# One small fp32 product of the identity (16 columns) in front of runs of feature-major products

## What is computed

```python
# first block, for each of 2 layers
z = rmsnorm(x, norm1_g[i]) @ w_in[i] + b_in[i]          # mq, mk, mv, mo, ..., rq, rk, rv, rg, gm, gr
merged = sigmoid(gm) * (y_m @ w_bm[i]) + sigmoid(gr) * (y_r @ w_br[i])
x = x + merged @ w_out[i]
h2 = rmsnorm(x, norm2_g[i])
x = x + square(relu(h2 @ w_ff1[i] + b_ff1[i])) @ w_ff2[i] + b_ff2[i]
# second block, expert part, for each of 2 layers; 128 * 128 experts
q = (x @ w_q).reshape(B, T, 8, 2, 64)
s = einsum('bthcd,hcnd->bthcn', q, sub_keys)
top_s, top_i = top_k(s, 16); best_s, pos = top_k(all pairs of sums, 16)
h = gelu(x @ exp_u[idx]); out = (softmax(best_s) * h) @ exp_v[idx]
```

## Time and profile before

| | |
|---|---|
| median of 3 runs | 3293.87 us (3293.05 to 3303.98) |
| span of the profiled execution | 3294.1 us |
| TensorE busy | 3190.2 us, 97% |
| VectorE busy | 2158.7 us, 66% |
| ScalarE busy | 1499.6 us, 46% |
| mean granted clock of TensorE | 0.988 |
| DMA | 565.12 MB, mean 172 GB/s |

### The profile page before, as it was taken

One profiled execution on the slowest core, in us unless ns is written; L12 is line 12 of the kernel. 1 busy time (PEld: TensorE's weight loads), 2 busy tenths in 40 slices (PEclk: granted clock), 3 DMA queues, 4 the chain that ended last, 5 costly groups with the idle time before them and its releaser, 6 DMA issues.

```text
span 3294.1 us, 49471 instructions
## 1 busy us (share of the span) xinstructions
PE 3190.2 (97%) x20642; PEld 2822.8 (86%) x20642; DVE 2158.7 (66%) x3111; ACT 1499.6 (46%) x1717; POOL 504.0 (15%) x278
## 2 busy tenths in 40 slices
PE   8999999999999999989999999999999989999998
PEld 7797889797977897877999989888769989989887
DVE  6775665577766655675987755555687977655555
ACT  6444454463434545613444444444344444444443
POOL 0000000000000000010866600000004856300000
PEclk9999999999999999999999999999999999999999
DMA  5454645444545454303544475555424544565553
GB/s 219 157 190 164 225 170 192 155 157 173 192 166 205 179 191 181 116 28 116 179 164 155 145 257 191 192 193 195 173 90 152 182 141 154 203 219 191 192 192 127
DMA packets 87656, 565.12 MB, mean 172 GB/s; under 512 B 10192, under 2 KB 10208, under 8 KB 23568
## 3 DMA queue, kind: packets, MB, share of 16 engines
q1 hardware_dynamic: 80496, 534.81, 45.4%
q0 software_dynamic: 6944, 27.21, 2.5%
HBM read 552.54 MB, written 9.44 MB: 171 GB/s over the span
## 4 chain that ended last, share of the span: by engine, by line
PE 45%; DVE 13%; ACT 2%; issue 1%; DVEq 0%; ACTq 0%
PE bank L2006 14%; PE bank L2033 7%; PE bank L2034 7%; PE bank L2038 7%; PE bank L1987 3%; DVE hid L2774 1%; DVE hid L2737 1%; PE bank L1730 1%; PE bank L1704 1%; PE bank L1731 1%; PE bank L1710 1%; PE bank L1705 1%; PE bank L1738 1%; DVE topi L2743 1%; DVE topi L2734 1%
## 5 line engine op out<-in xcount | busy, mean ns | idle before, releaser
L2162 ACT ACTIVATE w_hi<-raw 128x2048 fp32r<-128x2048 f32 x291 | 557.7, 1917 | 746.1 <-PE bank L2038 376.6
L2439 DVE TENSOR_TENSOR w_lo<-raw,w_hi 128x2048 fp32r<-128x2048 f32 x222 | 508.7, 2292 | 549.2 <-ACT w_hi L2162 548.4
L987 DVE TENSOR_TENSOR w_lo<-raw,w_hi 128x2048 fp32r<-128x2048 f32 x200 | 458.1, 2292 | 337.3 <-ACT w_hi L748 336.0
L748 ACT ACTIVATE w_hi<-raw 128x2048 fp32r<-128x2048 f32 x201 | 384.8, 1916 | 454.1 <-PE bank L521 316.5
L2006 PE MATMUL bank<-act_hi,w_hi 128*128 128x256 f32 x2048 | 497.8, 284 | 0.0
L2006 PE MATMUL bank<-act_lo,w_hi 128*128 128x256 f32 x2048 | 493.1, 282 | 0.0
L2033 PE MATMUL bank<-w_hi,c_hi 128*128 128x512 f32 x1024 | 398.6, 389 | 0.0
L2034 PE MATMUL bank<-w_hi,c_lo 128*128 128x512 f32 x1024 | 398.6, 389 | 0.0
L2006 PEld LDWEIGHTS bank<-act_lo,w_hi 128*128 128x128 f32 x2048 | 389.4, 190 | 0.1
L2006 PEld LDWEIGHTS bank<-act_hi,w_hi 128*128 128x128 f32 x2048 | 389.3, 190 | 0.1
L1627 POOL TENSOR_TENSOR w_lo<-raw,w_hi 128x2048 fp32r<-128x2048 f32 x70 | 332.5, 4757 | 335.3 <-ACT w_hi L2162 174.0
(11 more groups left out here) (507 smaller groups left out, 5299.5 us busy)
## 6 DMA issues: line engine op xcount, KB each, us to landing
raw<-weights SPq DMA_DIRECT2D x492, 1024.0 KB, 4.8
row<-rows POOLq DMA_DIRECT2D x48, 256.0 KB, 4.2
spill<-staged SPq DMA_DIRECT2D x32, 256.0 KB, 3.0
hid<-spill SPq DMA_DIRECT2D x32, 256.0 KB, 4.9
y<-w_pe POOLq DMA_DIRECT2D x2, 1024.0 KB, 5.1
ln_row_mix<-ln_rows POOLq DMA_DIRECT2D x4, 512.0 KB, 4.9
hid<-keys POOLq DMA_DIRECT2D x2, 1024.0 KB, 6.2
ln_row_ffn<-ln_rows POOLq DMA_DIRECT2D x4, 512.0 KB, 6.7
```

The source lines that it names most:

```text
L748: nc.scalar.activation(w_hi[:, k % SPLIT, :], raw[:, k % RAW, :], ACT.Copy).then_inc(hi_ready, 1)
L987: nc.vector.tensor_tensor(w_lo[:, k % SPLIT, :], raw[:, k % RAW, :], w_hi[:, k % SPLIT, :].bitcast(F32), ALU.subtract).then_inc(lo_ready, 1)
L2162: A.activation(hi_of(k), raw[:, k % RAW, :], ACT.Copy).then_inc(hi_ready, 1)
L2439: V.tensor_tensor(lo_of(k), raw[:, k % RAW, :], hi_of(k).bitcast(F32), ALU.subtract).then_inc(lo_ready, 1)
```

## The change

A helper `lead_in` is added in both blocks. It issues one fp32 product: the identity as the stationary operand, its first 16 columns as the moving one, written to the first 16 columns of a PSUM bank. It waits for nothing and signals nothing. It stands before `rqk` and before `ffb1` in each layer of the first block; in the expert part before the first `hidden` run of layer 0 alone, and before the late `hidden` run (pairs 48 to 63) in both layers. Counted as executed that is seven.

```diff
+            def lead_in(bank):
+
+                nc.tensor.matmul(psum[bank][:, 0:16], ident, ident[:, 0:16], start=True, stop=True)
+
...
                 nat("bm", 1, mix_hi, mix_lo)
+                lead_in(4)
                 for i in range(4):
                     feat("rqk", i, act_hi, act_lo)
...
                 for half, (one, two) in enumerate((("ffa1", "ffa2"), ("ffb1", "ffb2"))):
+                    if half:
+                        lead_in(4)
                     for i in range(4):
                         feat(one, i, act_hi, act_lo, by_bank(T_H2) if half == 0 and i == 0 else None)
...
+            if layer == 0:
+                lead_in(7)
             for p in range(HELD):
                 hidden(p)
...
             for o in range(EARLY):
                 output(o)
+            lead_in(7)
             for p in range(HELD, EXPERT_PAIRS):
                 hidden(p)
```

## The result

The changed kernel takes 3302.13 us, the median of 20 executions (3297.21 to 3305.5), against 3294.46 us for the kernel before, also of 20. The ratio is 1.0023, with a 95% interval of 1.0017 to 1.0030: 7.7 us slower, where 3284.4 was forecast in a range of 3279 to 3297. The time of an execution is its span and 1.8 us around it (after: 3301.48 for the profiled one, with a span of 3299.7), so the sum of the prediction starts from a span, which as a time is 3295.9. The medians of the kernel before are 3293.87 (3 executions) and 3294.46 (20), so this moves the forecast by under 2 us.

The account below looks back on a forecast made before the run. The stream of TensorE instructions was taken as the kernel's clock. From the profiled span, 3294.1 - 12.7 (six runs turned fast) + 1.9 (lead-ins) + 1.1 (lower clock after the seventh) = 3284.4 us, range 3279 to 3297.

Parts of the forecast that it names:

- the step that failed: At `rqk`, `ffb1` and late expert runs, both layers: lead-ins turn slow runs fast, gaining 12.7 us; chance 0.50.
- The six would go together: The six sites at `rqk`, `ffb1` and late experts have the same sequence before them, so mostly turn together.
- a time offset that it inherits: Claim that a run's pace comes from the sequence before it, not a coin toss at each execution; no size given.
- Cost of a lead-in: At each of the six sites: 0.31 us, from 0.22 for two records and 0.09 for the second step; sum 1.9.
- the lower bound of 0.22: Least cost of one lead-in at the six sites, its two records alone: 0.22 us, sum 1.3.
- The rival "nothing turns": No site turns and seven lead-ins are paid: 3296, or 3297 if only the first expert run turns; chance 0.20.
- The seventh: Lead-in before layer 0's first expert run: 5.1 us saved becomes waiting for the picks at L2049, gain zero.
- the price: Behind the longer wait at L2049 in layer 0, the clock stays low for longer: 1.1 us more.

Follow-up runs that it names:

- before (first four's): The kernel before, unchanged, run beside the first four follow-up kernels: 3294.54 us, median of 29 executions.
- before (the next three's): The kernel before, unchanged, run beside a later group of three follow-up kernels: 3293.09 us, median of 19 executions.
- before (the last two's): The kernel before, unchanged, run beside the last two follow-up kernels: 3295.55 us, median of 16 executions.

## Why the prediction was wrong

**The six sites don't turn (the step that failed).** The prediction took -12.7 us from the step "an fp32 product just ahead can let a run go fast, which no token-major product does", and gave it 0.50. Behind token-major products the change's lead-in gave the slow pace in 14 of 14 places (six in the change, six without the seventh, two before `rqk` alone), and in the six places with other widths and counts. The evidence for it was the third `mqk` chunk, one fast of two, the first expert runs, one fast of two, and the alternating gate pieces. I read an fp32 product in front as what sets the pace, where these rows show only that one doesn't exclude the fast pace. Over the traces without a lead-in there, that chunk is fast in 5 of 24 cases and the first expert runs in 8 of 24: the two halves that I counted were draws. A row that was there, and that I didn't weigh, was the fourth `mqk` chunk: behind transposes with 4 stationary columns it is fast in both layers of the kernel before, and in all 26 cases over the 13 traces. The experiment that alters only that width settles it for these sites. Why the width matters is not shown. The Trainium skill (TensorE: Matmul & The Clock Gate, LDWEIGHTS) says that the time of a weight load goes by the columns of the stationary operand alone; the traces agree in direction, with records of 0.19 us for a load of 128 columns and 0.08 for one of 4. One mechanism suggests itself: a short load leaves the stream of loads idle for a moment ahead of the run, as a pause does. The loads speak against it. With one transpose in front the last load ends at 187.92 us and that of the run begins at 188.07; with two records of 4 columns it is 186.31 and 186.35, in the kernel before 186.16 and 186.20. Idle for 0.15, 0.04 and 0.04 us, these runs go fast, fast and slow.

**The six would go together.** Right, in both directions: six slow in the change, six fast with the narrow products. "The pace seems fixed by the sequence, from a time offset that it inherits" holds at these six for what stands in front. An offset is not borne out there: six widths and counts of lead-in gave one pace.

**Cost of a lead-in.** Forecast 0.31 us, measured 0.37 + 45.19 against 0.23 + 45.11, that is 0.22, and 0.22 at the late runs as well. The two records put the first product of the run 0.14 us later, not 0.22, and the second step adds 0.08. So the lower bound of 0.22 came out, by another sum. Six are 1.3 us, not 1.9.

**What the sum left out.** `rv` takes 0.83 us more in each layer and `ffb2` 0.05. I had looked only for gains behind the sites. With 6 x 0.22 + 2 x 0.83 + 2 x 0.05 the sites cost 3.1 us. The rival "nothing turns" had 3296 to 3297 from 1.9 for the lead-ins and 1.1; with 3.1 on the median of 3294.46 it would be 3297.6, and 3302.1 was measured; 4.6 us are left.

**The seventh.** Right in its steps, with the price too high: 130.6 us, a wait that goes from 2.2 to 8.4 (7.3 was forecast), a mean clock of 0.82 behind it instead of 0.84 (10.82 us against 10.59, where 1.1 us more was forecast, so +0.2). Alone it is worth nothing: 0.9998. What the prediction didn't see is that this run takes either pace without any lead-in: it was fast in 4 of 11 traces, with the change's lead-in in 2 of 2. At that rate two of two come by chance about one time in eight, so whether the lead-in turned it is not shown, and that the forecast came true may be luck.

**The 4.6 us beyond the sites.** Each execution has a span and a mean granted clock. The span times what the clock lacks to 1 is called here the time lost at the lower clock. It is an upper bound: in the 13 traces 28 to 44 us are lost so, and TensorE is idle for 5 to 10 of them, in waits that a full clock would not shorten. For the same reason the rest is only roughly what the span would be without it. The clock is given to three digits, so each value is good to some 1.6 us, and means over many executions to less (± is one standard error):

| kernel | executions | lost at the lower clock | the rest of the span |
|---|---|---|---|
| before (first four's) | 29 | 35.4 ± 0.6 | 3258.1 ± 0.3 |
| the change | 20 | 40.8 ± 0.6 | 3259.6 ± 0.3 |
| the seventh alone | 11 | 35.9 ± 0.7 | 3257.7 ± 0.5 |
| the six alone | 11 | 38.4 ± 0.9 | 3260.8 ± 0.6 |
| the two before `rqk` | 12 | 39.6 ± 1.1 | 3259.0 ± 0.2 |
| before (the next three's) | 19 | 35.2 ± 0.8 | 3256.4 ± 0.5 |
| six, 4 stationary columns | 9 | 37.6 ± 0.8 | 3246.3 ± 0.5 |
| six, one transpose each | 5 | 36.1 ± 3.0 | 3245.2 ± 0.9 |
| that at more places | 10 | 36.8 ± 0.8 | 3245.8 ± 0.6 |
| before (the last two's) | 16 | 34.0 ± 0.8 | 3259.6 ± 0.5 |
| shift alone | 11 | 36.9 ± 0.8 | 3261.0 ± 0.5 |
| one transpose each, `rv` too | 5 | 32.8 ± 1.1 | 3247.7 ± 0.6 |

Each row is to be set against the kernel before of its own group, whose rest differs by up to 3.2 us from group to group. Beside the change itself no clocks of the kernel before are on record; against the first group, 5.4 of the 6.9 us between the mean spans are lost at the lower clock and 1.5 are in the rest. With the six alone, inside one group, it is 2.9 ± 1.1 and 2.7 ± 0.7, and the 2.7 fit the 3.1 us of the sites. The loss is there with the two lead-ins before `rqk` alone (4.2 ± 1.2), and not with the seventh alone.

The two profiled executions don't show it: by their clock rows 39.9 us are lost in the kernel before and 38.2 in the change, both at a mean of 0.988. What they show is how such time moves about: `rqk` of layer 0 starts at 186.46, as before, and the first expert run of layer 0 at 1574.75, 8.6 us late, of which the sites ahead of it are 4 x 0.22 + 2 x 0.83 + 2 x 0.05 = 2.6 and `ffa1` of layer 0 is 1.7; the other 4.3 lie between these. The stretch from the end of `rv` to `ffa1` of layer 0 took 163.0 us at a clock of 1.00 and now takes 164.8 at 0.99, and the one from 1301 us to the first expert run 265.0 and now 266.9, both at 0.97. Part of the 8.6 is given back later: in layer 1 the first expert run is 5.1 us longer, but the wait behind it is 6.2 shorter and the stretch behind the wait 2.6 shorter, at a clock of 1.00 and not 0.76. At the end 5.6 are left, of which the sites are 3.1 and `ffa1` 1.7. The kernel that only shifts the work by 0.86 us in each layer loses 2.9 ± 1.1 us in the same way, so a shift may do a part of it. That it does all of it isn't shown: two standard errors to each side of 2.9 reach from 0.7 to 5.1. What the lead-ins before `rqk` do to the clock further on, and with it the cause of the 4.6 us, stays open.

**The range.** Its upper end, 3297, was the rival's time with bounds of its own costs, and had nothing for the cost of pauses that fall otherwise against the clock, though two timed executions of the same kernel lay 10 us apart.

## What to carry to other kernels

Where long runs of equal products have no gap, compare the distance of their products between runs before looking for waits: 113.5 against 117.8 ns, over six runs, was 12 to 13 us by the lengths of the runs and 7 to 12 by the medians of the kernels here. A transpose with 4 stationary columns (0.02 us) in front of a run that follows other products at the full clock took it, where a product with 128 stationary columns didn't. An example in the trace in which something "sometimes" goes along with the good case is no mechanism; look for the place where it always does, and copy that, with all its shapes. And 5.2 us gained in front of a wait for another engine were worth nothing.

## What was not expected of the hardware

- Feature-major products of 256 moving columns, with a weight load each, have two stable mean distances at a granted clock of 1.00, 113.5 and 117.8 ns, and a run of 384 products or more keeps the one that it takes in its first products. The Trainium skill (TensorE: Matmul & The Clock Gate, Back-to-back issue gap) has one distance for a width: for 256 columns 262 cycles as the isolated gap, and for streams of loads and products figures at 128 and 512 columns only. No run here agrees with that: there are two distances, and both are above the 109 ns of 262 cycles at 2.4 GHz.
- Token-major products of 512 columns have at least two mean distances in one and the same run: 229.0 and 233.3 ns in `rv`. It was 233.3 each time that a product with 128 stationary columns stood in front of `rqk`, 384 products earlier (8 of 8), and 43.72 to 43.81 us for the run otherwise.
- The pace of a run behind a wait differs between executions: `ffa1` is at the fast one in 16 of 24. In layer 1 it is fast in the kernel before and slow in the one with the seventh alone, which has the same instructions up to there. The run `k`, which begins at the lower clock behind other products, is fast in 8 of 12.
- The first expert run of layer 0 doesn't fit the rule of the six sites: behind the change's lead-in of 128 stationary columns it was fast in 2 of 2, and without it in 4 of 11. There fp32 products of 256 columns stand in front, not token-major ones. Why is not settled.
- A gain at the sites needn't arrive whole. By the sites' own lengths six runs at the fast pace are 11.6 us with the fp32 product and 12.9 with the transpose. The medians differ by 7.4 and 9.4, by 8.5 with the transposes at more places, and by 12.0 with one before `rv` too. In the table the rest of the span falls by 10.1 to 11.9 us in these four, while the time at the lower clock goes from 2.4 ± 1.1 us more to 1.2 ± 1.3 less.
